# Delta rule outputs token-major, last gate unit after the recurrence, memory attention padded, decay and rotary work moved between engines

## The reference, cut to what matters

```python
diff = g_cum[..., :, None] - g_cum[..., None, :]
decay = where(causal, exp(where(causal, diff, 0.0)), 0.0)
t_mat = where(strict, (k * beta) @ k.T * decay, 0.0) + eye
u = solve(t_mat, v * beta);  w = solve(t_mat, k * beta * exp(g_cum))
qk = (q @ k.T) * decay
# per chunk: v_new = u - w @ state
#            out   = (q * exp(g_cum)) @ state + qk @ v_new
#            state = state * d + k_dec.T @ v_new
o = rms_norm(o, out_gain) * silu(gate)          # gated output of layer A
x = x + concat([o_a, o_m]) @ w_out              # o_m: memory attention
# layer B
q_rope = [x1 * cos - x2 * sin, x1 * sin + x2 * cos]
```

## Time and profile before

| what | us |
|---|---|
| median of three runs | 1243.8 (1242.74 to 1245.93) |
| the profiled execution, its time | 1242.98 |
| the profiled execution, its span | 1241.2 |
| mean granted TensorE clock, of full speed | 0.992 |

### The profile page before, as it was taken

The page is one execution under the profiler, slowest core; times in us unless marked ns, Lnnn a source line. Parts: engine busy times, 40 slices in busy tenths (PEclk is TensorE's granted clock), DMA queues, the critical chain, the costliest instruction groups (busy, mean ns, idle before and its releaser), DMA issues.

```text
span 1241.2 us, 22479 instructions
## 1 busy us (share of the span) xinstructions
PE 1216.3 (98%) x7938; PEld 1105.3 (89%) x7938; DVE 945.4 (76%) x1622; ACT 744.6 (60%) x1200; POOL 99.8 (8%) x106
## 2 busy tenths in 40 slices
PE   7999999999999998999999999999999999999997
PEld 7899999888888998989888888988888989888886
DVE  7675789988866888567887866888876777888853
ACT  7454656777744677456777645666654556666642
POOL 4660000000000024400000000000000010000000
PEclk9999999999999999998999999999999999999998
DMA  9534545555663344113454743555664423555720
GB/s 352 195 116 176 207 164 176 198 181 200 217 226 136 136 162 153 35 35 136 169 203 172 261 177 110 196 192 180 219 232 138 142 88 111 195 196 182 262 106 34
DMA packets 48773, 209.90 MB, mean 169 GB/s; under 512 B 3366, under 2 KB 5812, under 8 KB 44228
## 3 DMA queue, kind: packets, MB, share of 16 engines
q1 hardware_dynamic: 47648, 205.55, 46.7%
q10 hardware_dynamic: 1060, 3.48, 0.8%
HBM read 207.93 MB, written 1.10 MB: 168 GB/s over the span
## 4 chain that ended last, share of the span: by engine, by line
PE 89%; DVE 8%; ACT 1%; issue 1%; DMA 1%; DVEq 0%; ACTq 0%
PE main L1998 25%; PE main L2269 13%; PE main L2000 13%; PE main L1971 7%; PE main L1973 7%; PE main L2271 7%; PE main L1972 7%; DVE w_lo L1047 2%; DVE cy L1481 2%; PE side L2078 1%; PE main L2426 1%; PE side L2052 1%; PE main L2301 1%; PE side L2301 1%; PE main L2608 1%
## 5 line engine op out<-in xcount | busy, mean ns | idle before, releaser
L1047 DVE TENSOR_TENSOR w_lo<-raw,w_hi 128x1024 fp32r<-128x1024 f32 (+3 forms) x365 | 468.6, 1292 | 7.9 <-ACT w_hi L556 7.1
L1998 PE MATMUL main<-xg,w_hi 128*128 128x512 f32 x1344 | 470.2, 393 | 0.3 <-DVE w_lo L1047 0.2
L556 ACT ACTIVATE w_hi<-raw 128x1024 fp32r<-128x1024 f32 (+2 forms) x363 | 402.2, 1110 | 84.5 <-PE main L1973 62.9
L2000 PE MATMUL main<-xg,w_lo 128*128 128x256 f32 x1344 | 376.9, 280 | 0.0
L1998 PEld LDWEIGHTS main<-xg,w_hi 128*128 128x128 f32 x1344 | 252.3, 188 | 58.1 <-DVE w_lo L1047 0.6
L2000 PEld LDWEIGHTS main<-xg,w_lo 128*128 128x128 f32 x1344 | 252.5, 188 | 0.1
L2269 PE MATMUL main<-h_both,w_hi 128*128 128x512 f32 x704 | 247.9, 394 | 0.4
L2271 PE MATMUL main<-h_both,w_lo 128*128 128x256 f32 x704 | 199.1, 283 | 0.0
L1971 PE MATMUL main<-xg,w_hi 128*128 128x256 f32 (+1 forms) x656 | 191.0, 291 | 1.3 <-DVE xg L1081 0.9
L1972 PE MATMUL main<-xg,w_lo 128*128 128x256 f32 (+1 forms) x656 | 185.5, 283 | 0.0
L1973 PE MATMUL main<-xg,w_hi 128*128 128x256 f32 (+1 forms) x656 | 185.5, 283 | 0.0
(11 more groups left out here) (454 smaller groups left out, 1652.2 us busy)
## 6 DMA issues: line engine op xcount, KB each, us to landing
raw<-in_w_gu_a SPq DMA_DIRECT2D x44, 1024.0 KB, 5.2
raw<-in_w_gu_b SPq DMA_DIRECT2D x44, 1024.0 KB, 5.2
raw<-in_w_down_a SPq DMA_DIRECT2D x16, 1408.0 KB, 6.2
raw<-in_w_down_b SPq DMA_DIRECT2D x16, 1408.0 KB, 6.1
raw<-in_w_in SPq DMA_DIRECT2D x15, 1024.0 KB, 5.4
raw<-in_w_in_a SPq DMA_DIRECT2D x13, 1024.0 KB, 5.2
raw<-in_w_gates SPq DMA_DIRECT2D x4, 1024.0 KB, 5.2
raw<-in_w_up SPq DMA_DIRECT2D x4, 1024.0 KB, 5.2
```

What stands on the lines that cost most here:

```text
L556: act.activation(w_hi[:, u % RING, 0:n], raw[:, s % RAW, u % 2, 0:n], ACT.Copy).then_inc(hi_ready, 1)
L1047: return dve.tensor_tensor(dst, src, hi.bitcast(F32), ALU.subtract)
L1998: pe.matmul(bank[:, :], piece(w_hi, u, k), xg[:, :, k, 0:SEQ], start=k == 0, stop=k == KC - 1, skip_group_check=True)
L2000: ins = pe.matmul(bank[:, 0:SEQ], piece(w_lo, u, k), xs_hi[:, k], start=False, stop=k == KC - 1, skip_group_check=True)
```

## The change

- Decays: ScalarE makes |difference| with Abs and a bias (12 operations, t = 11 to 13), one exponential for three heads at t = 18, no masks before it; GpSimd instead masks the products `a_t` after `grams`. The transfer that feeds it is issued two passes earlier (t = 8), its source one pass earlier (t = 7). The sums that the grams wait for move one pass earlier on VectorE.
- Grams: heads 1 and 2 at t = 18, 3 at t = 19, 4 and 5 at t = 20; `pack` uses a predicated copy and adds the identity on VectorE, and the two identity products go.
- Unit 24 takes unit 25's place around `first_level`; unit 25 (the last gate) is projected after the recurrence, in two halves.
- The delta rule's outputs come token-major, are squared and summed on ScalarE and VectorE, scaled, and turned by 12 transposes; then one operation applies gain and gate.
- Memory attention's products use all 128 rows and 128 columns, over zeros.
- Rotary: ScalarE copies the raw queries, VectorE does the products with cos and the sum.

(Indentation is cut by two levels below.)

```diff
...
-        if t == 8:
+        if t == 7:
...
-        if t == 10:
+        if t == 8:
...
+        if 11 <= t < 14:
+            if t == 11:
+                act.wait_ge(spread_in, 16)
+                act.wait_ge(col_copied, 3)
+            for h in (2 * t - 22, 2 * t - 21):
+                for c in range(2):
+                    ins = act.activation(dec[:, h, c * P:(c + 1) * P], spread[:, h, c * P:(c + 1) * P],
+                                         ACT.Abs, bias=g_col[:, c, h:h + 1], scale=-1.0)
+            if t == 13:
+                link(ins)
...
+        if t in (7, 8):
+            for i in range(2):
+                ins = act.activation(v_pad_a[t - 7][:, :, 128 * i:128 * i + 64],
+                                     heads_apart(mem_v[:, 0, t - 7, :])[:, :, i, :], ACT.Copy)
+            ins.then_inc(v_padded, 1)
+        if t == 17:
+            act.wait_ge(csum, 12)
+            act.activation(k_odd[64:P, :, :], mem_k[64:P, 0, :, :], ACT.Copy).then_inc(k_moved, 1)
...
-        for h in {18: (0,), 19: (1, 2), 20: (3,), 21: (4, 5)}.get(t, ()):
-            act.wait_ge(diff_ready, h + 1)
-            act.activation(dec[:, h, 0, :], dec[:, h, 0, :], ACT.Exp, scale=-1.0)
-            act.activation(dec[:, h, 1, :], dec[:, h, 1, :], ACT.Exp).then_inc(decay_ready, 1)
-            if h == 3:
-                act.wait_ge(diff_ready, DH)
-                act.activation(spread[:, :, P:SEQ], spread[:, :, P:SEQ], ACT.Exp).then_inc(late_ready, 1)
+        if t == 18:
+            for g in range(GROUPS):
+                act.activation(dec[:, heads_of(g), :], dec[:, heads_of(g), :], ACT.Exp, scale=-1.0)\
+                   .then_inc(decay_ready, 1)
+            act.activation(spread[:, :, P:SEQ], spread[:, :, P:SEQ], ACT.Exp).then_inc(late_ready, 1)
...
+            act.wait_ge(rec_pe, 11 + j)
+            ins = act.activation(rhs1[:, heads, :], by_three(rec[2 + j]), ACT.Square)
+        ins.then_inc(o_squared, 1)
...
-    slot(u0 + 25)
...
-    act.wait_ge(rec_dve, 12)
-    square_outputs(1)
+    act.activation(root[:, 0:1], one_c, ACT.Sqrt, bias=eps_c)
+    for j in range(2):
+        square_outputs(1, j)
+    act.wait_ge(o_summed, 2)
+    act.activation(o_inv[:, 1, :], o_sum[:, 1, :], ACT.Sqrt).then_inc(o_root_done, 1)
     copy_pt(MEM_A + 3)
...
+    gate(0)
...
-    act.wait_ge(og_dve, 1)
-    act.activation(o_inv, cols[:, 208:220], ACT.Sqrt).then_inc(o_root_done, 1)
+    gate(1)
+    slot(u0 + 25)
     act.wait_ge(evac, in_tile(25) + 1)
...
-        act.activation(cat_hi_a[:, 2 * j:2 * j + 2, :], o_a[:, 2 * j:2 * j + 2, :], ACT.Copy)\
+        if j == 1:
+            gate(2)
+        act.wait_ge(o_gated, j + 1)
+        act.activation(cat_hi_a[:, 2 * j:2 * j + 2, :], gate_a[:, 2 * j:2 * j + 2, :], ACT.Copy)\
...
     slot(r0)
+    for i in range(3):
+        if i < 2:
+            act.wait_ge(unit_used, r0 + i + 1)
+        act.activation(q_raw[:, i, :], main[(FIRST_TILE["qrope"] + i) % 4][:, 0:SEQ], ACT.Copy)\
+           .then_inc(raw_copied, 1)
...
-        dve.tensor_tensor(both, both, by_three(turn_bank(g)), ALU.add).then_inc(second_ready, 1)
+        dve.copy_predicated(both, causal.bitcast(I32).unsqueeze(1).to_broadcast([P, 3, P]),
+                            by_three(turn_bank(g))).then_inc(second_ready, 1)
         dve.wait_ge(second_ready, g + 1)
-        dve.tensor_tensor(inv_c[:, g, :, :], both, level_mask(0), ALU.mult).then_inc(c_first, 1)
+        link(dve.tensor_tensor(inv_c[:, g, :, :], both, level_mask(0), ALU.mult))
+        dve.tensor_tensor(inv_c[:, g, :, :], inv_c[:, g, :, :], ident.unsqueeze(1).to_broadcast([P, 3, P]),
...
+            grams(2 * (t - 18))
+            grams(2 * (t - 18) + 1)
+        if t in (21, 22):
+            pack(t - 21)
+        if t == 23:
...
                .then_inc(rec_dve, 1)
+    def sum_outputs(c):
+
+        for j in range(2):
+            dve.wait_ge(o_squared, 2 * c + j + 1)
+            squares = rhs1[:, 3 * j:3 * j + 3, :] if c else k_dec[j][:, :, :]
+            ins = dve.tensor_reduce(o_square[:, c, 3 * j:3 * j + 3], squares, AX.X, ALU.add)
+            ins.then_inc(o_reduced, 1)
+        dve.wait_ge(o_reduced, 2 * c + 2)
+        dve.scalar_tensor_tensor(o_sum[:, c, :], o_square[:, c, :], 1.0 / DK, q_eps[:, c, :], ALU.mult, ALU.add)\
+           .then_inc(o_summed, 1)
...
     row_maxima(MEM_A + 3)
+    sum_outputs(0)
...
     slot(u0 + 25)
+    sum_outputs(1)
+    dve.wait_ge(o_root_done, 1)
+    dve.reciprocal(o_inv[:, 1, :], o_inv[:, 1, :]).then_inc(o_inv_ready, 1)
+    dve.wait_ge(o_inv_ready, 1)
     for j in range(2):
-        by_heads(o_a[:, :, P:SEQ], rec[2 + j], j, 11 + j)
+        heads = slice(3 * j, 3 * j + 3)
+        dve.tensor_tensor(o_t[:, 1, heads, :], by_three(rec[2 + j]),
+                          o_inv[:, 1, heads].unsqueeze(2).to_broadcast([P, 3, P]), ALU.mult).then_inc(rec_dve, 1)
     take_output(om_a[:, 1, :], MEM_A + 3)
...
+        pair = gate_a[:, 2 * j:2 * j + 2, :]
+        dve.wait_ge(o_turned, j + 1)
+        dve.wait_ge(gate_silu, j + 1)
+        dve.scalar_tensor_tensor(pair, turned_bank(j)[:, :].rearrange("p (h n) -> p h n", h=2),
+                                 par[:, C_OUTG:C_OUTG + 1], pair, ALU.mult, ALU.mult).then_inc(o_gated, 1)
+
+    def output_lo(j):
+        dve.wait_ge(cat_hi_ready, 2 + j)
...
-
-
-    dve.wait_ge(og_pe, 1)
-    dve.scalar_tensor_tensor(o_sum, side[3][:, 0:12].rearrange("p (c h) -> p c h", c=2), 1.0 / DK, q_eps,
...
-        dve.wait_ge(og_pe, 3 + j)
-        dve.scalar_tensor_tensor(pair, pair, par[:, C_OUTG:C_OUTG + 1],
-                                 scale_bank(j)[:, :].rearrange("p (h n) -> p h n", h=2), ALU.mult, ALU.mult)\
-           .then_inc(og_dve, 1)
-        if j > 0:
...
-        dve.wait_ge(gate_silu, j + 1)
-        dve.wait_ge(og_dve, 3 + 2 * j)
-        dve.tensor_tensor(pair, pair, gate_a[:, 2 * j:2 * j + 2, :], ALU.mult).then_inc(og_dve, 1)
+    unit_done(u0 + 25)
+    taken(gate_a[:, 5, :], in_tile(25), rstd[:, 0:SEQ]).then_inc(evac, 1)
+    gated_output(1)
+    output_lo(0)
+    gated_output(2)
+    output_lo(1)
...
     row_maxima(MEM_B + 3)
-    split_lo(out0 + 1)
...
     gp.wait_ge(consts_set, 3)
     half = half_c.to_broadcast([P, 12]).rearrange("p (c h) -> p c h", c=2)
-    gp.wait_ge(spread_in, 16)
-    gp.wait_ge(col_copied, 3)
+    gp.wait_ge(sums_ready, 1)
+    gp.tensor_tensor(k_root, sums[:, :, 0:6], half, ALU.pow).then_inc(root_done, 1)
+    for i in range(2):
+        gp.memset(v_pad_a[i][:, :, 64:P], 0.0).then_inc(k_padded, 1)
+    gp.wait_ge(csum, 12)
...
-                              spread[:, h, :].rearrange("p (c n) -> p c n", c=2),
-                              g_col[:, :, h:h + 1].to_broadcast([P, 2, P]), ALU.subtract))
-        link(gp.tensor_tensor(dec[:, h, 1, :].rearrange("p (c n) -> p c n", c=2),
-                              dec[:, h, 0, :].rearrange("p (c n) -> p c n", c=2),
-                              const[:, K_CAUS:K_CAUS + P].unsqueeze(1).to_broadcast([P, 2, P]), ALU.add))
-        gp.tensor_tensor(dec[:, h, 0, :].rearrange("p (c n) -> p c n", c=2),
-                         dec[:, h, 0, :].rearrange("p (c n) -> p c n", c=2),
-                         const[:, K_ANTI:K_ANTI + P].unsqueeze(1).to_broadcast([P, 2, P]), ALU.add)\
-          .then_inc(diff_ready, 1)
-        if h == 2:
-            gp.wait_ge(sums_ready, 1)
-            gp.tensor_tensor(k_root, sums[:, :, 0:6], half, ALU.pow).then_inc(root_done, 1)
+        gp.wait_ge(n_ready, h + 1)
+        gp.tensor_tensor(a_t[:, 2 * h:2 * h + 2, :], a_t[:, 2 * h:2 * h + 2, :],
+                         causal.unsqueeze(1).to_broadcast([P, 2, P]), ALU.mult).then_inc(a_masked, 1)
...
+
     gp.wait_ge(evac, FIRST_TILE["krope"] + 1)
     gp.memset(k_rope[64:P, 0, :], 0.0).then_inc(cleared, 1)
     gp.memset(k_rope[0:64, 1, :], 0.0).then_inc(cleared, 1)
+    gp.wait_ge(cleared, 2)
...
+                                 heads_apart(mem_v[:, 1, c, :])[:, :, i, :])
+    ins.then_inc(cleared, 1)
+    gp.wait_ge(cleared, 4)
     gp.wait_ge(evac, FIRST_TILE["in_b"] + 1)
...
-                     ALU.mult).then_inc(rope_cos, 1)
-    gp.wait_ge(evac, FIRST_TILE["qrot"] + 3)
-    gp.wait_ge(rope_cos, 1)
-    gp.tensor_tensor(q_rope[:, :, :], q_rope[:, :, :], rot_s[:, :, :], ALU.add).then_inc(rope_ready, 1)


 @block.tensor
...
                 h = a - MEM_A
-                r = slice(64 * (h % 2), 64 * (h % 2) + 64)
-                ins = pe.matmul(dst, qm_a[r, h // 2, q], mem_k[r, 0, h // 2, :], start=True, stop=True)
+                k = k_odd[:, h // 2, :] if h % 2 else mem_k[:, 0, h // 2, :]
...
-                h, layer = (a - MEM_A, 0) if which == "mem_a" else (a - MEM_B, 1)
-                v = mem_v[:, layer, key // P, h * 64:h * 64 + 64]
+                h = (a - MEM_A) % MEMH
+                v_pad = v_pad_a[key // P] if which == "mem_a" else v_pad_b[:, key // P]
+                v = v_pad[:, h // 2, 64 * (h % 2):64 * (h % 2) + P]
             q = (2 - first) * P
```

(74 more changed lines are left out.)

175 lines of the change are left out of this document (93 added, 82 removed).

## The result

The changed kernel took 1228.8 us (median of 4: 1226.9, 1227.0, 1230.7, 1230.7) against 1243.4 us before (median of 4, 1242.7 to 1245.9). The ratio is 0.9878, 95% interval [0.9862, 0.9893]: 14.6 us, or 1.2%, less. The forecast was 1235.3 us, with a range of 1231.5 to 1241.5. The direction was right; 6 us more were gained than I had summed, and the range did not hold the time. The profiled execution took 1230.7 us (span 1229.0, granted clock 0.993), so it is one of the two longer ones; those of 1227 us had a clock of 0.996, and 0.003 × 1229 = 3.7 us is the difference between them.

A forecast was written before the change was run, and what follows sets the result against it. TensorE, busy 98% of the span, was taken to bound the kernel, through products, waits and clock. Terms 2.3 + 1.3 − 2.1 + 0.4 + 0.2 + 5.2 + 1.2 = 8.5 us off 1243.8 gave 1235.3 us, range 1231.5 to 1241.5.

The forecast's parts named there:

- Part 1: Projection up to the unit with `first_level`: wait for sums goes, head 3 waits 4.4 us; gain 2.3 us, bounds 0.3 and 8.4.
- Part 2: Start of the inversion: identity products go, gain 1.3 us; ScalarE's late copy of the packed product loses 2.1 us.
- Part 4: Behind the recurrence, to the fourth output tile: 16.6 instead of 21.8 us; gain 5.2 us, bounds 0.3 and 6.
- the chain of squares and roots: Behind the recurrence, the new norm work on the other engines: ends by 552.5 us, when TensorE reaches the transposes.
- The items named for it: Behind the recurrence: 4.9 us clock, 2.8 one-column products, some 1.5 spreading, less 2.9 for the unit and 1.45 for transposes.
- Rival A: Start of the inversion: clock falls after 2.1 us idle, costing 2 to 5 us, about 1238.5 us; chance 0.19.
- a low clock anywhere but after head 3's wait: Sign in the profile after: if the clock column is low elsewhere, the forecast is wrong.
- Part 3: Padding of memory attention: gain 0.4 us for four heads' scores and 0.2 us for the outputs.
- Part 5: Layer B: VectorE freed of slow scalings beside GpSimd, normalisation wait goes; gain 1.2 us, bounds 0 and 1.6.
- rival C: Projection: VectorE relieved in full, head 0 wait shrinks to 2 us, clock holds; about 1231 us; chance 0.09.

The follow-up runs named there:

- after_order: Changed kernel with one ScalarE weight split moved from before the copies of the packed product to behind the inversion's first level: 1225.1 us, ratio 0.9848.
- experiment 5: Last gate unit back before the inversion, in the changed kernel with three wait edits: 1223.0 us; kernel before with 2 instead of 24 one-column products: 1242.2 us.
- experiment 4: Changed kernel with one ScalarE split later: 1225.1 us; grams of heads 3 and 5 one unit later: 1224.6; decay exponentials at t = 13: 1224.3; all three: 1221.4.
- before_few_sums: Kernel before with 2 instead of 24 one-column products behind the recurrence (output not the reference's): 1242.2 us, ratio 0.9982.
- Experiment 1: Everything from `free0` on placed 32 bytes higher in SBUF: in the kernel before 1241.1 us (ratio 0.9975), in the changed kernel 1232.1 us (0.9902).

## Why the prediction was right, and where it was wrong

**Right.** The mechanism of Part 1 came out almost to the tenth: tile 18 taken at 475.20 (forecast 475.2), head 3's gram at 481.7 (481.5), the wait 3.8 us (4.4), none for the sums. VectorE's weight splits took 1.22 us between t = 12 and 17, as forecast, and 1.64 us beside GpSimd's new masks (482.74). The unit with `first_level` began at 500.24 instead of 499.2: 0.2 us of it lie in head 3's start, and 0.8 in the clock, of which about 2.5 us were lost behind the wait instead of 1.7. The transposes of `ba`, which moved one unit forward as well, now wait 0.8 us at 443 us for VectorE's scan; I had not looked for this wait, but it lies ahead of the one for head 3, whose end the other engines set, so it does not explain the later start. Part 2's wait for `inv_f` was 1.9 us (2.1), with the cause that I named; after_order shows it. Part 4 took 15.8 us (forecast 16.6), at full clock, and the chain of squares and roots ended at 550.4, before TensorE asked at 550.9. Why the clock stays up there, the largest term of my sum, is not shown by any run (experiment 5), so of that term the size was right and its reason is open. The items named for it add up to 4.85 us and not to the 5.2 that came from the difference of the two stretches.

**Rival A came true, in the profiled execution.** Behind the wait for `inv_f` the clock was 0.64 from 508 to 512 us, at a price of 1.7 us (experiment 4). I had given this 0.19, and had named a low clock anywhere but after head 3's wait as a sign that the forecast is wrong. That executions of one kernel differ by such stretches was not in my sum, which took one profile's time for the median's: the profile after lies 1.9 us above its median and the one before 0.5 below, together 2.4 of the 6 us. I also counted the low stretch at 479 to 486 us of the kernel before as 1.7 us lost; before_few_sums shows it cost nothing there.

**Wrong: the terms that were too small.** First, a term was missing. The sum held only what the edits do to instructions and waits; the shift of `free0` was worth some 3.1 us, 2.9 of them in the down-projections, and my sum had no term for it. Experiment 1 shows it from both sides. Second, Part 3 was mis-sized. "Four score instructions take 1.06 us with 64 rows and 0.96 us with 128" counted a group by itself, with a row in which the neighbours' shapes were already others, and for the outputs I took 0.2 of at most 0.8 us. The runs say 3.6 to 4.0 us instead of 0.6, since each change between 64 and 128 rows or columns costs 0.14 to 0.19 us, the change back to the unpadded groups behind as much as the one before. The Trainium skill (TensorEngine Tiling (Array Packing), Key Properties) says that a change of tiling mode, unlike one of tile, drains TensorE; the chain rows above fit this, with 1.53 against 1.34 us for 12 unchanged products. Third, Part 5 was worth 1.95 to 2.6 us alone, where I had 1.2 with 1.6 as the upper bound. I had added up the waits of TensorE; around the one of 1.1 us the stage gained 1.54, and the short wait for `rot_s` behind it was worth 0.46 where I had counted 0.2. The rest, up to the 1.95, is not resolved. Part 4 lay 0.8 us above its estimate, at its upper bound.

**Why the range failed.** Its lower end came from rival C, relief of VectorE, which did not happen. Nothing in it stood for several terms being too small at once, nor for an effect on code that the diff leaves alone. From the table, 2.9 (addresses) + 1.4 (recurrence) + 0.8 (tail) + 2.0 (layer B) − 2.1 (inversion) − 0.3 (Part 1) − 0.8 (start) − 0.2 (rest) = 3.7 us separate 8.5 from 12.2.

## What to carry to other kernels

An edit that changes the length of anything in SBUF also changes the distances between matmul operands behind it: compare the duration of an untouched stage in both traces before crediting the edit, and when a stage is long, try the four distances of 32 bytes. Price a change of tile shape by its neighbours in the chain of waits, not by the group itself. And a long wait of TensorE is to be priced twice, with and without a low stretch behind it; moving one split and the grams of two heads by one unit took most of both waits away here. Before a low stretch is put down as lost, look whether TensorE has to wait right behind it all the same.
